# A decoder trunk with 32 streamed experts on one core: gate/up fills of the middle experts in pairs of 4 MB

## What is computed

```python
logits = xt @ w_router + b_router            # 256 tokens, 32 experts
top_v, top_e = top_k(logits, 4); gate = softmax(top_v)
# for each expert e, on the tokens that chose it:
gu = xb @ w_gate_up[e] + b_gate_up[e]        # (1024, 2048): 8 MB
g, u = min(gu[:, :1024], 7), clip(gu[:, 1024:], -7, 7)
hmid = (u + 1) * (g * sigmoid(1.702 * g))
y[tok] += gate * (hmid @ w_down[e] + b_down[e])   # (1024, 1024): 4 MB
```

## Time and profile before

| what | value |
|---|---|
| median of 3 runs | 1214.55 us |
| the profiled execution's own time | 1215.05 us |
| its span | 1213.3 us |
| TensorE busy | 1129.4 us (93%) |
| VectorE, ScalarE busy | 304.9, 224.7 us |
| moved by DMA | 445.49 MB, 44297 packets |
| weight fills | 192 of 2 MB |

### The profile page before, as it was taken

One profiled execution on the slowest core, in us unless ns is written; L12 is line 12 of the kernel. 1 busy time (PEld: TensorE's weight loads), 2 busy tenths in 40 slices (PEclk: granted clock), 3 DMA queues, 4 the chain that ended last, 5 costly groups with the idle time before them and its releaser, 6 DMA issues.

```text
span 1213.3 us, 12721 instructions
## 1 busy us (share of the span) xinstructions
PE 1129.4 (93%) x5426; PEld 494.1 (41%) x5427; DVE 304.9 (25%) x700; ACT 224.7 (19%) x451; POOL 36.2 (3%) x34
## 2 busy tenths in 40 slices
PE   6999899999999999999999999989999999999897
PEld 5886675555333333333333333333333333333332
DVE  4777552214112211111121111111111111111111
ACT  5674462243001000000010000000000000000002
POOL 0000050040000000000000000000000000000000
PEclk9999899999999999999999999999999999999999
DMA  8824433387999999999999999999999999999995
GB/s 350 311 82 150 128 139 136 109 349 304 428 429 426 429 427 427 428 427 429 426 428 428 427 427 428 428 428 426 428 427 429 427 429 426 428 427 428 428 427 228
DMA packets 44297, 445.49 MB, mean 367 GB/s; under 512 B 6064, under 2 KB 10256, under 8 KB 19440
## 3 DMA queue, kind: packets, MB, share of 16 engines
q1 hardware_dynamic: 42096, 444.37, 87.9%
q10 hardware_dynamic: 2144, 0.30, 0.2%
HBM read 443.60 MB, written 1.05 MB: 366 GB/s over the span
## 4 chain that ended last, share of the span: by engine, by line
PE 57%; DMA 36%; DVE 3%; ACT 2%; issue 1%; SPq 0%; DVEq 0%; ACTq 0%
DMA R<-in_w_gate_up 21%; PE ps L1949 17%; PE ps L1958 13%; DMA XM<-in_w_gate_up 7%; PE ps L1814 5%; PE ps L1466 4%; PE ps L1978 4%; DMA XMT<-in_w_gate_up 3%; DMA QK<-in_w_down 3%; PE ps L1925 3%; PE ps L1486 2%; PE ps L1488 2%; PE ps L1487 2%; PE ps L1720 2%; PE ps L1940 1%; DMA A<-in_w_xkv 1%
## 5 line engine op out<-in xcount | busy, mean ns | idle before, releaser
L1949 PE MATMUL ps<-R,convT 128*64 128x512 f32 x1248 | 279.2, 596 | 22.5 <-DMA R<-in_w_gate_up 22.3
L1369 DVE TENSOR_SCALAR A<-ps 128x512 f32<-128x512 f32 x30 | 20.7, 692 | 648.9 <-PE ps L1949 648.9
L1949 PEld LDWEIGHTS ps<-R,convT 128*64 128x64 f32 x1248 | 86.9, 137 | 202.5 <-issue 153.6
L1958 PE MATMUL ps<-R,A 128*64 128x512 f32 x592 | 131.3, 592 | 0.0
L875 ACT ACTIVATE A<-A 128x512 f32<-128x512 f32 x30 | 18.9, 630 | 474.7 <-DVE A L1369 474.7
L1958 PEld LDWEIGHTS ps<-R,A 128*64 128x64 f32 x592 | 41.4, 137 | 76.7 <-issue 75.3
L1978 PE MATMUL ps<-A,convT 64*128 64x512 f32 x248 | 61.6, 615 | 0.7 <-ACT A L882 0.7
L1925 PE MATMUL ps<-H,convT 128*64 128x512 f32 x256 | 60.4, 592 | 0.3 <-DVE convT L1324 0.3
L882 ACT COPY A<-ps 128x512 f32<-128x512 f32 x30 | 17.6, 586 | 221.3 <-PE ps L1958 221.3
L1949 PE MATMUL ps<-XM,convT 128*64 128x512 f32 x208 | 47.0, 594 | 3.7 <-DMA XM<-in_w_gate_up 3.7
L1949 PE MATMUL ps<-QK,convT 128*64 128x512 f32 x208 | 47.0, 594 | 3.3 <-DMA QK<-in_w_gate_up 3.3
(11 more groups left out here) (317 smaller groups left out, 1215.7 us busy)
## 6 DMA issues: line engine op xcount, KB each, us to landing
R<-in_w_gate_up SPq DMA_DIRECT2D x78, 2048.0 KB, 40.8
R<-in_w_down SPq DMA_DIRECT2D x36, 2048.0 KB, 42.7
QK<-in_w_gate_up SPq DMA_DIRECT2D x13, 2048.0 KB, 40.8
XM<-in_w_gate_up SPq DMA_DIRECT2D x13, 2048.0 KB, 43.0
A<-in_w_gate_up SPq DMA_DIRECT2D x12, 2048.0 KB, 40.8
XMT<-in_w_gate_up SPq DMA_DIRECT2D x12, 2048.0 KB, 42.2
QK<-in_w_down SPq DMA_DIRECT2D x7, 2048.0 KB, 40.5
A<-in_w_down SPq DMA_DIRECT2D x7, 2048.0 KB, 43.1
```

Source lines behind the costliest of these rows:

```text
L1949: last = mm(bank(b)[s * SLOTS:(s + 1) * SLOTS, :], xg[:, 4 * (j % 2) + 2 * c + j // 2, :], w[:, c * 2 * FF + at + s * BANK:c * 2 * FF + at ...
L1958: last = mm(bank(o)[s * SLOTS:(s + 1) * SLOTS, :], h[:, c, i * SLOTS:(i + 1) * SLOTS], w[:, c * D + s * BANK:c * D + (s + 1) * BANK], star ...
```

## The change

The tiles `XM` and `A` become one tile `XA`, so that the slots can be put in another order: `R` 0 to 3, `XM`, half of `A`, `R` 4 and 5, `QK`, `XMT`. Four pairs of neighbouring slots are now contiguous in a partition: 0-1, 2-3, 4-5, 6-7. Slots 8 and 9 are not.

For experts 2 to 29 ("wide") a half of the gate/up matrix (512 rows, 4 MB) is laid out as four consecutive rows per partition, 32 KB in one run. If the pair of slots is contiguous, it is one transfer of 4 MB; else two of 2 MB, each with 16 KB runs at a distance of 32 KB. SP waits until both slots are free. TensorE waits for the one semaphore of the pair, and adds to `freed` after each half as before. The row order differs, so there is a second form of the token transposes, of the matmuls' left operand and of the gain columns (`R_XW`, eight more columns of `prm`, made by eight small matmuls near the start).

On SP the stream now begins right after the loads of `w_o2`: fills 0 to 3; then the wait for q, the bias loads and the wait for the output transposes; fill 4; fill 5 after `act_part` 3; 6 and 7 after `pe_xo` 3 and 4; 8 without a wait of its own; 9 as before.

```diff
-        ring = ([QK[:, :]] + [R[:, f * 4096:(f + 1) * 4096] for f in range(4)] + [XM[:, :]]
-                + [R[:, f * 4096:(f + 1) * 4096] for f in (4, 5)] + [A[:, 0:4096], XMT[:, :]])
+        R_slot = [R[:, f * 4096:(f + 1) * 4096] for f in range(6)]
+        ring = R_slot[0:4] + [XM, A[:, 0:4096]] + R_slot[4:6] + [QK[:, :], XMT[:, :]]
+        PAIR = {0: R[:, 0:8192], 2: R[:, 8192:16384], 4: XA[:, 0:8192], 6: R[:, 16384:24576]}
...
+        def wide(k):
+            return 2 <= k < A_EXP
...
+            if n < FILLS * A_EXP and wide(k) and n % FILLS < GU_FILLS and n % 2 == 1 and slot - 1 in PAIR:
+                ARRIVAL[n] = ARRIVAL[n - 1]
...
-                sp.wait_ge(pe_two, TWO["q", 1])
-                for part in range(3):
-                    sp.dma_start(b_raw[part * E:(part + 1) * E, 0:2 * FF], b_gate_up[0]).then_inc(ld_bias, 16)
-                    sp.dma_start(b_raw[part * E:(part + 1) * E, 2 * FF:BW], b_down[0]).then_inc(ld_bias, 16)
...
+                def wide_rows(k, h):
+                    return w_gate_up[0, k:k + 1, h * 4 * P:(h + 1) * 4 * P, :].rearrange("o (p c) n -> p (o c n)", c=4)
...
+                    if n == 4:
+                        sp.wait_ge(pe_two, TWO["q", 1])
+                        for part in range(3):
+                            sp.dma_start(b_raw[part * E:(part + 1) * E, 0:2 * FF], b_gate_up[0]).then_inc(ld_bias, 16)
+                            sp.dma_start(b_raw[part * E:(part + 1) * E, 2 * FF:BW], b_down[0]).then_inc(ld_bias, 16)
+                        sp.wait_ge(pe_two, TWO["oT", 1])
                     if n == 5:
-                        sp.wait_ge(pe_two, TWO["oT", 1])
+                        sp.wait_ge(act_part, 3)
                     if n in (6, 7):
                         sp.wait_ge(pe_xo, n - 3)
-                    if n == 8:
-                        sp.wait_ge(act_part, 3)
                     if n == 9:
                         sp.wait_ge(pe_lg, T)
+                    if wide(k) and j < GU_FILLS:
+                        if j % 2 == 0:
+                            slot = ring_slot(k, j)
+                            sp.wait_ge(freed, n - RING + 2)
+                            if slot in PAIR:
+                                sp.dma_start(PAIR[slot], wide_rows(k, j // 2)).then_inc(arrived[slot], 16)
+                            else:
+                                for h in range(2):
+                                    sp.dma_start(ring[slot + h], wide_rows(k, j // 2)[:, 4 * FF * h:4 * FF * (h + 1)]
+                                                 ).then_inc(arrived[slot + h], 16)
+                        continue
...
-                link(V.tensor_copy(prm[:], bank(7)[:, 0:R_END + KC]), dve_prm)
+                link(V.tensor_copy(prm[:], bank(7)[:, 0:R_END + 2 * KC]), dve_prm)
...
+                xg_wide = xg_rows.rearrange("j (n c) -> j c n", c=4)
+                for c in range(4):
+                    for b in range(2):
+                        mm(bank(7)[b * 64:(b + 1) * 64, R_XW + 2 * c:R_XW + 2 * c + 2], xg_wide[:, c, :],
+                           ident[0:4, 0:4].rearrange("p (a b) -> p b a", b=2)[:, b, :], start=True, stop=True)
...
+                def gather_transposes_wide():
+                    rows = hmf.rearrange("p (n c) -> p c n", c=4)
+                    for c in range(4):
+                        last = tr(bank(U_BANK)[:, c * P:(c + 1) * P], rows[:, c, :])
+                    return last
...
-                        pe.wait_ge(arrived[ring_slot(k, j)], ring_at(k, j))
-                        gate_up(j, xgT, ring[ring_slot(k, j)]).then_inc(freed, 1)
+                        await_fill(pe, k, j)
+                        (gate_up_wide(j, ring[ring_slot(k, j)]) if wide(k) else gate_up(j, xgT, ring[ring_slot(k, j)])).then_inc(freed, 1)
```

More of the change, by code:

```diff
@@ L41 @@
 NEG = -1e30
-R_MIX, R_XA, R_MEM, R_MOE, R_NSA, R_CNV, R_B1, R_CW, R_POS, R_END, R_XG = 0, 8, 16, 24, 32, 36, 40, 44, 56, 88, 88
+R_MIX, R_XA, R_MEM, R_MOE, R_NSA, R_CNV, R_B1, R_CW, R_POS, R_END, R_XG, R_XW = 0, 8, 16, 24, 32, 36, 40, 44, 56, 88, 88, 96
 def links(eng, default):
@@ L80, in trunk @@
             R_p = parts("R_p", [P, 24576])
-            XM_p, MK_p = parts("XM_p", [P, 4096]), parts("MK_p", [P, 2048])
+            XA_p, MK_p = parts("XA_p", [P, 12288]), parts("MK_p", [P, 2048])
             convT_p = parts("convT_p", [P, 1024])
-            A_p, H_p, XMT_p = parts("A_p", [P, 8192]), parts("H_p", [P, T * D]), parts("XMT_p", [P, 4096])
+            H_p, XMT_p = parts("H_p", [P, T * D]), parts("XMT_p", [P, 4096])
             QK_p = parts("QK_p", [P, 4096])
         R = sb("R", [P, 24576])
-        XM = sb("XM", [P, 4096])
+        XA = sb("XA", [P, 12288])
         MK = sb("MK", [P, KC, S])
         convT = sb("convT", [P, CC, S])
-        A = sb("A", [P, 8192])
         H = sb("H", [P, T, D])
@@ L92, in trunk @@
         QK = sb("QK", [P, 4096])
-        for part, whole in ((QK_p, QK), (R_p, R), (XM_p, XM), (MK_p, MK), (convT_p, convT), (A_p, A), (H_p, H), (XMT_p, XMT)):
+        for part, whole in ((QK_p, QK), (R_p, R), (XA_p, XA), (MK_p, MK), (convT_p, convT), (H_p, H), (XMT_p, XMT)):
             assert nc.lookup_mloc(part).addr == nc.lookup_mloc(whole).addr
+        XM, A, XM_p, A_p = XA[:, 0:4096], XA[:, 4096:12288], XA_p[:, 0:4096], XA_p[:, 4096:12288]
         XS_p, MV_p = XM_p[:, 0:2048], XM_p[:, 2048:4096]
@@ L113, in trunk @@
         prm_rows = sb("prm_rows", [R_END, P])
-        prm = sb("prm", [P, R_END + KC])
+        prm = sb("prm", [P, R_END + 2 * KC])
         ones = sb("ones", [P, 1])
@@ L390, in ring_slot, with await_fill @@
             return fill_no(k, j) % RING
-        def ring_at(k, j):
-            return 16 * (fill_no(k, j) // RING + 1)
+        def wide(k):
+            return 2 <= k < A_EXP
+        ARRIVAL = {}
+        landed = [0] * RING
+        for n in range(FILLS * E):
+            slot, k = n % RING, n // FILLS
+            if n < FILLS * A_EXP and wide(k) and n % FILLS < GU_FILLS and n % 2 == 1 and slot - 1 in PAIR:
+                ARRIVAL[n] = ARRIVAL[n - 1]
+            else:
+                landed[slot] += 16
+                ARRIVAL[n] = (slot, landed[slot])
+        def await_fill(eng, k, j):
+            slot, count = ARRIVAL[fill_no(k, j)]
+            eng.wait_ge(arrived[slot], count)
         LAST_TWO = ([(A_EXP, j) for j in range(GU_FILLS)] + [(B_EXP, j) for j in range(GU_FILLS)]
@@ L1330, in build_selg, with xg_out @@
                         yield V.tensor_scalar(dst[:, t, :], iot, keys[:, t, c], gtab[:, t, c], ALU.is_equal, ALU.mult)
-                def xg_out(dst):
+                def xg_out(dst, row=R_XG):
                     return V.tensor_tensor(dst, bank(U_BANK).rearrange("p (m n) -> p m n", m=KC),
-                                           prm[:, R_XG:R_XG + KC].unsqueeze(2).to_broadcast([P, KC, SLOTS]), ALU.mult)
+                                           prm[:, row:row + KC].unsqueeze(2).to_broadcast([P, KC, SLOTS]), ALU.mult)
                 def col(e):
@@ L1378, in expert @@
                         dve.wait_ge(m_xT, k + 2)
-                        xg_out(xgT).then_inc(m_xg, 1)
+                        xg_out(xgT, R_XW if wide(k + 1) else R_XG).then_inc(m_xg, 1)
                     dve.wait_ge(m_sgT, k + 1)
@@ L1949, in gate_up, with gate_up_wide @@
                                 last = mm(bank(b)[s * SLOTS:(s + 1) * SLOTS, :], xg[:, 4 * (j % 2) + 2 * c + j // 2, :],
+                                          w[:, c * 2 * FF + at + s * BANK:c * 2 * FF + at + (s + 1) * BANK], start=False,
+                                          stop=(j == 3 and c == 1), skip_group_check=True)
+                    return last
+                def gate_up_wide(j, w):
+                    for c in range(2):
+                        for b, at in ((G_BANK, 0), (U_BANK, FF)):
+                            for s in range(2):
+                                last = mm(bank(b)[s * SLOTS:(s + 1) * SLOTS, :], xgT[:, 2 * (2 * (j % 2) + c) + j // 2, :],
                                           w[:, c * 2 * FF + at + s * BANK:c * 2 * FF + at + (s + 1) * BANK], start=False,
@@ L2015, in expert @@
                         pe.wait_ge(m_swi, 2 * k + 1)
-                        gather_transposes().then_inc(m_xT, 1)
+                        (gather_transposes_wide() if wide(k + 1) else gather_transposes()).then_inc(m_xT, 1)
                     pe.wait_ge(m_h, k + 1)
```

1 line of the change is left out of this document (added).

## The result

The changed kernel takes 1217.64 us in the median of 20 runs (1215.64 to 1219.11) beside 1214.42 for the kernel before; the ratio is 1.0026, with an interval of 1.0019 to 1.0033. That is 3.2 us slower; the prediction said 2.9 us (1217.4). One of the 20 executions of the kernel before took 2368 us and is left out of the ratio. The number was right, in part by luck. Two of its terms were wrong and nearly cancelled: the longer runs gained more than twice what I gave them, and a delay on TensorE that I had put at nothing took the difference back.

What follows compares the result with a forecast made beforehand. DMA was taken to bound the kernel from the first expert on. Small matmuls +1.0, holes +3.3 and longer runs -1.4 summed to +2.9 us, 1217.4 against 1214.55; range 1212 to 1221.

Steps and rivals of the forecast that it cites:

- Order of the first fills: Stream start, first ten fills: nothing late for expert 0, fill 10 still hangs on `freed`; cost and gain 0.
- Small matmuls: Near the start on TensorE: eight small matmuls delay everything that follows, `freed` too; +1.0 us (0 to 2.6).
- Both slots: Early stream: waiting for both slots makes holes of 0.6 us at pair 12/13 and 2.7 at 14/15; +3.3 us.
- Longer runs: Wide experts' stream: one packet less per 32 KB in 45 pairs, at 3.9 ns each; -1.4 us (0 to -4.2).
- The other end of my range: Longer runs' gain priced at 11.8 ns per packet, from 2 and 4 KB runs: 4.2 us.
- The estimate from the ceiling: Stream: if all missing to the 435 GB/s fabric ceiling were paid per packet, 10.8 ns each, 3.9 us gained.
- Pairs in the steady part: Wide experts and hand-over to 30 and 31: DMA keeps the pace, TensorE still waits for fills 188 to 191; 0 us.
- rival D: Hand-over to experts 30 and 31: pair landings make TensorE late, up to 3.4 us more, +6.3 in all; chance 0.07.
- The sign that I named for it: For the late-TensorE rival: holes after 350, or TensorE idle in experts 30 and 31 with DMA done.
- S: Whole kernel: the prediction's own sum, 1.0 front, 3.3 holes, 1.4 gained, with the end set by DMA.

Runs made afterwards that it cites:

- e11: Changed kernel with no wide experts and without the eight small matmuls; only slot order and first-fill order new: 1214.35 us, ratio 1.0000.
- e2: Changed kernel, but wide from expert 4 on instead of 2: 1214.83 us, ratio 0.9997.
- e12: e8 measured again, beside e11 on the same chip: 1211.54 us, ratio 0.9977.
- e8: Changed kernel, wide only for experts 4 to 27, without the eight small matmuls, gain columns loaded by two transfers instead: 1211.55 us, ratio 0.9980.
- e5: As e4, but each pair goes as two 2 MB transfers with 16 KB runs: 1216.12 us, ratio 1.0017.
- e6: As e4, but each pair is one 4 MB transfer with two 16 KB runs per partition, old row order: 1216.24 us, ratio 1.0021.
- e3: Changed kernel, but wide up to expert 27 instead of 29: 1215.57 us, ratio 1.0014.
- e10: Changed kernel, but expert 29 gets its pairs as two transfers each, so each half lands by itself: 1215.95 us, ratio 1.0014.
- e9: The changed kernel itself measured once more, on another chip: 1218.14 us, ratio 1.0029.
- e7: Changed kernel with eight idle 128x128 matmuls on TensorE before it waits for the second pair of expert 29: 1216.82 us, ratio 1.0022.
- e4: Changed kernel, but wide only for experts 4 to 27: 1213.36 us, ratio 0.9990.

## Why the prediction was right, and which steps were not

**Order of the first fills, 0:** right. e11 is at the time of before, within 1.1 us.

**Small matmuls, +1.0:** their price was right to 0.05 us (1.05 in the chain). What reaches fill 10 is 0.55 in the changed kernel's profile, but 0.3 to 2.1 us over the ten profiles with them (299.67 subtracted), 1.5 in the mean against the four without. Part of the scatter is there before them: they start at 35.78 to 37.13. In the three with the earliest fill 10 (before 300.3) the chain has no wait for `w_xkv`, in the other seven it has one, which ends at 119 to 120; the cause wasn't followed.

**Both slots, +3.3:** right in place and size. 3.0 by e2. The Trainium skill's remark on DMA Optimizations (Perfetto Trace Analysis), that smaller pieces may start sooner, held here for those two pairs and for none later.

**Longer runs, -1.4: mis-sized.** I priced a packet by the rows nearest in length, 4 and 16 KB, at 3.9 ns. e12 against e11 gives 2.8 us for 39 pairs, 8 packets fewer per engine in each: 9.0 ns per packet, 3.2 us for 45 pairs (their profiles, from fill 10 to fill 190, give 3.0 us, that of e8 2.7). The other end of my range had 11.8. The estimate from the ceiling in the Trainium skill (DMA: Bandwidth & Descriptors, Bandwidth), 10.8 ns and 3.9 us, was nearer than my choice; e5 and e6 agree with its assumption that the cost is one per packet. Rates over 6 us of a transfer among others were too rough to be divided into nanoseconds: 418 and 421 for the same run length are 1.1 ns apart, and by one or the other alone the result is 4.7 or 3.2 ns.

**Pairs in the steady part, 0: this step failed.** I wrote that TensorE "enters them about 1 us later than before and waits for fills 188 to 191 anyway". I had worked out the drift from one wide expert to the next, which a wait wipes out, and not the hand-over to the single ones. There, TensorE has 3.4 us more to do after the last landing, and 1.7 more where the clock falls in the 2.1 us wait: 5.1 us in the profile. TensorE enters expert 30 5.0 us later than before (1155.73 and 1150.73), not about 1. The room in experts 30 and 31 was smaller. From the landing at 1131.0 to the end of the down fills the kernel before needs 72.9 us, waits included, the changed one 75.4 with 5.1 us more of work: so there were some 2.7 us of waits and slow stretches to give up, and the rest, 2.5 us, is the later end. e3 (2.1) and e10 (2.2) measure it. It is rival D, which I gave 0.07 and 3.4 us. The sign that I named for it was the wrong one: TensorE isn't idle in experts 30 and 31, it works there without a wait for data.

Together: 1.5 + 3.0 - 3.2 + 2.2 = +3.5 us, beside 3.2 measured at first and 4.1 in e9, whose seven runs spread from 1215.68 to 1218.45. So 1217.4 came out right since the gain was too small by 1.8 us and the end by 2.2; that these two cancel was luck. S was the right number from a wrong account: where a landing sets the end again, with 42 or 43 long transfers and both holes, the kernel is 1.0 (e3) to 1.9 us (e10) slower than before, not 2.9.

Left open: what share of the late end is the clock's (e7 didn't tell), why the front scatters by 2 us among kernels with the small matmuls, why e4's fill 190 lands late, and whether the 9 ns are the packet's own or come from reading 32 KB in one piece (both changed together).

## What to carry to other kernels

Where a stream sets the pace and another engine has some 8% to spare (here 26.9 us of work in 29.4), a delay of that engine is free only while a later wait can absorb it: look for the last such wait before the end, and count what the engine still has to do after the last coarse landing. Make the pieces coarse in the middle of the stream and single at both ends, where the queue is short and where the consumer must finish; here that turned +3.2 us into -1.2 (e4_both), and with the small matmuls out as well into -2.6 (e8_best). Before you read a gain of 1 us out of two medians, see in the profiles whether the part ahead of it took the same time. When a cost per packet decides, take it from long stretches, not from windows of a few us.

## What the hardware showed that I had not expected

- A packet of 32 KB saves about 9 ns over two of 16 KB on each DMA engine (e12 against e11: 2.8 us by the medians, 3.0 by the profiles, for 39 transfers), and a transfer of 4 MB in 16 KB runs saves nothing (e6).
- TensorE's clock: waits of 0.76 and 1.24 us between single fills left the granted clock at 2.4 GHz in this place (1.00 in 1126 to 1135, each fill 3.65 us); after a wait of 2.08 us for a pair the work ran partly at 1.2 GHz, 8.78 us in place of 7.09. It doesn't happen at each such wait: after 2.61 us at 922 us of the same profile the pair took the short time.

```profile
924.69 7.09 PE L2000 MATMUL ps<-XA,convT 128*64 128x512 f32 x32 [2.61 <-DMA XA<-in_w_gate_up]
...
953.96 8.79 PE L2000 MATMUL ps<-R,convT 128*64 128x512 f32 x32 [2.13 <-DMA R<-in_w_gate_up]
```

- The DMA engines seem not to end together: in the kernel before their mean share is 0.59, 0.57 and 0.42 in the three stretches from 1194 to 1200, and the other kernels' last 6 us look alike (0.65, 0.55 and 0.49 in e12). The 246 GB/s of the first of them are what about nine of 16 engines would move if all 16 move 428 (an estimate); no row here shows an engine alone.
